# Two attention layers, a gated FFN, a convolution and state space mixer, cross attention and an FFN in one kernel: segment sums by DMA instead of matmul, and five changes of order

## The reference, cut to what matters

```python
# one layer's attention (8 heads of 64, one key and one value head)
proj = rms_norm(x, g) @ w_in            # q, k, v, gates, index queries and keys, ...
score = sum_h(relu(q_idx[h] @ k_idx.T) * w_idx[h])       # w_idx is 8 columns beside v
sel = the 64 best visible keys of each query
p = softmax(where(sel, q @ k.T / 8, -inf));  out = p @ v

# mixer, state space half (32 heads of 64, 4 groups, state 128, chunks of 128)
xbc = silu(causal_dwconv(xbc, conv_w) + conv_b)          # 4 taps, 3072 channels
dt = softplus(dt_raw + dt_bias);  acs = cumsum(dt * a)   # per head, per chunk
decay = exp(acs[l] - acs[s]) for s <= l                  # 128 x 128 per head and chunk
y = (C @ B.T * decay) @ (x * dt) + exp(acs) * (C @ state)
```

## Time and profile before

| | |
|---|---|
| three executions | 1267.33, 1271.03, 1271.29 us, median 1271.03 |
| the profiled execution | 1270.99 us |
| its span | 1269.2 us |
| mean granted clock of TensorE | 0.995 of full speed |
| VectorE, ScalarE, POOL busy | 48%, 56%, 77% of the span |
| chain that ended last | TensorE 91%, VectorE 4%, ScalarE 2%, issue 1%, DMA 1% |
| HBM read, written | 206.07 MB, 1.05 MB |
| mean busy share of the DMA queue of the weights | 49.2% |

### The profile page before, as it was taken

One profiled execution on the slowest core, in us unless ns is written; L12 is line 12 of the kernel. 1 busy time (PEld: TensorE's weight loads), 2 busy tenths in 40 slices (PEclk: granted clock), 3 DMA queues, 4 the chain that ended last, 5 costly groups with the idle time before them and its releaser, 6 DMA issues.

```text
span 1269.2 us, 22533 instructions
## 1 busy us (share of the span) xinstructions
PE 1241.6 (98%) x8950; PEld 1141.5 (90%) x8950; DVE 609.7 (48%) x1489; ACT 716.0 (56%) x1347; POOL 978.8 (77%) x774
## 2 busy tenths in 40 slices
PE   6999999999999999999999999999999999999997
PEld 5899899998889888889999999999999888888886
DVE  4476754456656444422755666632135234444312
ACT  5455656465556666545554676674447446666532
POOL 4567658767568999989799766769889767899894
PEclk9999999999999999999999999999999999999999
DMA  6334335444345555555465444445556434555552
GB/s 233 124 126 158 131 129 183 152 148 150 117 135 192 188 183 190 190 181 186 150 200 200 150 134 136 151 147 180 179 176 223 157 125 157 184 190 191 173 194 81
DMA packets 57784, 208.58 MB, mean 164 GB/s; under 512 B 6352, under 2 KB 7632, under 8 KB 57552
## 3 DMA queue, kind: packets, MB, share of 16 engines
q1 hardware_dynamic: 57680, 207.15, 49.2%
HBM read 206.07 MB, written 1.05 MB: 163 GB/s over the span
## 4 chain that ended last, share of the span: by engine, by line
PE 91%; DVE 4%; ACT 2%; issue 1%; DMA 1%; SPq 0%; POOL 0%; DVEq 0%
PE bank L385 22%; PE bank L358 17%; PE bank L360 16%; PE bank L359 16%; PE bank L388 11%; PE bank L895 1%; PE bank L699 1%; PE bank L1789 1%; ACT whi L310 1%; PE bank L905 1%; DMA raw<-w_dram 1%; PE bank L2166 1%; PE bank L2138 1%; PE bank L837 1%; PE bank L2188 1%
## 5 line engine op out<-in xcount | busy, mean ns | idle before, releaser
L318 POOL TENSOR_TENSOR wlo<-raw,whi 128x512 fp32r<-128x512 f32 x770 | 978.6, 1300 | 275.1 <-ACT whi L310 273.3
L310 ACT ACTIVATE whi<-raw 128x1024 fp32r<-128x1024 f32 x387 | 404.3, 1053 | 33.5 <-DMA raw<-w_dram 11.8
L358 PE MATMUL bank<-xx,whi 128*128 128x256 f32 (+1 forms) x1296 | 378.9, 292 | 12.0 <-DVE xx L448 9.4
L360 PE MATMUL bank<-xx,wlo 128*128 128x256 f32 (+1 forms) x1296 | 368.8, 285 | 0.0
L359 PE MATMUL bank<-xx,whi 128*128 128x256 f32 (+1 forms) x1296 | 368.6, 284 | 0.0
L358 PEld LDWEIGHTS bank<-xx,whi 128*128 128x128 f32 x1296 | 246.4, 190 | 21.3 <-issue 11.7
L360 PEld LDWEIGHTS bank<-xx,wlo 128*128 128x128 f32 x1296 | 246.8, 190 | 0.0
L359 PEld LDWEIGHTS bank<-xx,whi 128*128 128x128 f32 x1296 | 246.3, 190 | 0.5
L385 PE MATMUL bank<-xx,whi 128*128 128x512 f32 x704 | 178.9, 396 | 0.0
L358 PE MATMUL bank<-yy,whi 128*128 128x256 f32 (+1 forms) x524 | 151.2, 289 | 0.0
L360 PE MATMUL bank<-yy,wlo 128*128 128x256 f32 (+1 forms) x524 | 148.9, 284 | 0.0
(11 more groups left out here) (276 smaller groups left out, 1412.8 us busy)
## 6 DMA issues: line engine op xcount, KB each, us to landing
raw<-w_dram SPq DMA_DIRECT2D x387, 512.0 KB, 3.3
h<-x_dram SPq DMA_DIRECT2D x2, 544.0 KB, 6.2
ar<-mem_dram SPq DMA_DIRECT2D x1, 1024.0 KB, 5.6
out_dram<-h SPq DMA_DIRECT2D x4, 256.0 KB, 2.2
cst<-con_dram SPq DMA_DIRECT2D x1, 721.0 KB, 9.6
cst<-con_dram SPq DMA_DIRECT2D x1, 134.0 KB, 3.4
prm<-par_dram SPq DMA_DIRECT2D x1, 131.0 KB, 3.2
```

Of the source, the lines that this page charges most:

```text
L310: e.activation(whi[:, i % NSPL, :], raw[:, i % NRAW, :], ACT.Copy).then_inc(*whi_done.done(i))
L318: return e.tensor_tensor(wlo[:, q, c0:c1], raw[:, i % NRAW, c0:c1], whi[:, q, c0:c1].bitcast(F), ALU.subtract)
L358: e.matmul(o, wh, both[:, 0, :], start=(i == 0), stop=False)
L360: m = e.matmul(o, wl, both[:, 0, :], start=False, stop=(i == len(feed) - 1))
```

## The change

The segment sums come by DMA: `acs` goes to a DRAM tensor of 32 by 256 (`sums`), and each pair of heads is read back from it with both rows spread over all 128 partitions (256 KB in SBUF), into one of three buffers `runs`, 16 loads in all, issued on ScalarE's queue. `E` is then made from that buffer into `E8`, ahead of the wait for the Relus, and the product with `C` is made in place in `E8`. The matmuls `seg`, `acr` and `idr` are gone. `taps` runs block by block, without interleaving; ScalarE has the tanh of the block before (`due`) ahead of its tick. In `attend_scalar` the copies stand ahead of the exponentials. In layer 0 the values' block precedes the keys'. `values_vector` yields six times instead of two.

```diff
 def values_vector(e, K):
         e.tensor_tensor(x[0:72, :], main.at("v", l)[0:72, 0:T], K.N.row[0:72, :], ALU.mult).then_inc(*v_out.done("v", l))
-        yield
-        yield
+        for _ in range(6):
+            yield
         w = K.V[:, 0:2, 64:72]
...
 def attend_scalar(e, K, t):
         for s in range(8):
-            for hh in (2 * s - 2, 2 * s - 1) if 1 <= s < 5 else ():
-                e.wait_ge(*v_step.of("max", l, t, s - 1))
-                e.activation(K.L[:, hh, 0:nk], K.L[:, hh, 0:nk], ACT.Exp, bias=K.nm[:, hh:hh + 1],
-                             accum_out=K.sm[:, hh:hh + 1]).then_inc(*s_step.done("exp", l, t, hh))
             for hh in (2 * s - 6, 2 * s - 5) if 3 <= s < 7 else ():
...
                 e.activation(pt[:, 1:nn, :], o[:, 128:128 * nn].rearrange("p (a b) -> p a b", b=128), ACT.Copy).then_inc(
                     *s_out.done("pt", l, t, hh))
+            for hh in (2 * s - 2, 2 * s - 1) if 1 <= s < 5 else ():
+                e.wait_ge(*v_step.of("max", l, t, s - 1))
+                e.activation(K.L[:, hh, 0:nk], K.L[:, hh, 0:nk], ACT.Exp, bias=K.nm[:, hh:hh + 1],
+                             accum_out=K.sm[:, hh:hh + 1]).then_inc(*s_step.done("exp", l, t, hh))
             yield
...
 def layer_tensor(e, K):
-        block(e, ("kk", l, 0), "w_in", l, [(512, 64, 0), (2688, 64, 64)], K.x_all, T, by=[(v_step, ("rope", l, "kk", 0))])
         if l:
+            keys_tensor(e, K)
             norm_sums(e, N)
         block(e, ("v", l), "w_in", l, [(576, 64, 0), (2752, 8, 64)], K.x_all, T)
         if l == 0:
+            keys_tensor(e, K)
             norm_sums(e, N)
...
+    def load_run(e, n):
+        if n < 16:
+            if n >= 3:
+                e.wait_ge(*s_step.of("fall", *divmod(n - 3, 4)))
+                e.wait_ge(*s_step.of("E", *divmod(n - 3, 4)))
+            e.dma_start(runs[n % 3], sums[2 * n:2 * n + 2, :].partition_broadcast(128)).then_inc(sems[f"run{n % 3}"], 16)
...
 def steps_scalar(e):
         e.wait_ge(*v_step.of("acs", 1))
+        e.dma_start(sums, acs).then_inc(sems["l_a"], 16)
         e.activation(dq[:, 0:128], acs[:, 0:128], ACT.Exp, scale=-1.0, bias=acs[:, 127:128]).then_inc(*s_step.done("dden"))
         yield
...
-        e.activation(acr[0:32, :], acs, ACT.Copy).then_inc(*s_high.done("acr"))
-        for i in (0, 1):
-            e.activation(idr[32 * i:32 * i + 32, :], ident[0:32, 0:32], ACT.Copy).then_inc(*s_high.done("idr", i))
+        e.wait_ge(sems["l_a"], 16)
+        for n in range(3):
+            load_run(e, n)
...
 def ssd_tensor(e, g):
         for hp in range(4):
-            o = side_.take(e, "seg", g, hp)
-            side_.give(("seg", g, hp), (v_step, ("EC", g, hp)))
-            e.wait_ge(*v_low.of("acr"))
-            for i in range(2):
-                hd = 8 * g + 2 * hp + i
-                m = e.matmul(o[:, S * i:S * i + S], idr[:, hd:hd + 1].broadcast_to([64, 128]), acr, start=True, stop=True)
-            m.then_inc(*piece.done("seg", g, hp))
             yield
...
 def ssd_vector(e, g):
                 e.wait_ge(*s_step.of("E", g, hp - 1))
-                e.tensor_tensor(E8[:, 2 * hp - 2:2 * hp, :], later(side_.at("seg", g, hp - 1)), ctb, ALU.mult).then_inc(
-                    *v_step.done("EC", g, hp - 1))
+                m = E8[:, 2 * hp - 2:2 * hp, :]
+                e.tensor_tensor(m, m, ctb, ALU.mult).then_inc(*v_step.done("EC", g, hp - 1))
...
 def ssd_scalar(e, g):
-            o = side_.at("seg", g, hp)
-            e.wait_ge(*piece.of("seg", g, hp))
+            n = 4 * g + hp
+            o = runs[n % 3]
+            e.wait_ge(sems[f"run{n % 3}"], 16 * (n // 3 + 1))
...
-            rise = later(o)
+            e.activation(E8[:, 2 * hp:2 * hp + 2, :], o[:, :, 128:256], ACT.Exp).then_inc(*s_step.done("E", g, hp))
             e.wait_ge(*s_step.of("fall", g, hp))
-            e.activation(rise, rise, ACT.Exp).then_inc(*s_step.done("E", g, hp))
             e.activation(M[:, 2 * hp:2 * hp + 2, :], M[:, 2 * hp:2 * hp + 2, :], ACT.Exp, scale=-1.0).then_inc(
                 *s_step.done("M", g, hp))
+            load_run(e, n + 3)
             yield
...
 def mixer_vector(e):
                     silu_vector(e, due)
                     due = ()
                     tick(side)
-                taps(e, pair)
-                due = pair
+                    taps(e, cb)
+                    due = (cb,)
...
 def mixer_scalar(e):
                     split_for(e, "cv", cb)
+                    silu_scalar(e, due)
+                    due = (cb,)
                     tick(side)
-                    silu_scalar(e, due)
-                    due = ()
-                due = pair
```

More of the change, by code:

```diff
@@ L227, in tick, with build @@
             side.remove(g)
-def build(tens, sems, known, wts, small, par, con, mem, out):
+def build(tens, sems, known, wts, small, par, con, mem, out, sums):
     P, V, A, G, Y = Tensor("pe"), Vector("dve"), Scalar("act"), Pool("pool"), Sync("sp")
@@ L1198, in mixed_low, with keys_tensor @@
                                ALU.subtract).then_inc(*v_low.done("mixed", l, g))
+    def keys_tensor(e, K):
+        l = K.l
+        block(e, ("kk", l, 0), "w_in", l, [(512, 64, 0), (2688, 64, 64)], K.x_all, T, by=[(v_step, ("rope", l, "kk", 0))])
     def layer_tensor(e, K):
@@ L1504, in build @@
     dtu, dtv, dtw = (M[0:32, i, :] for i in (0, 1, 2))
-    acr, idr = tens["acr"][:, 0:S], tens["acr"][:, S:S + 32]
+    runs = [sg[:, 2 * k:2 * k + 2, :] for k in range(3)]
     cwh, cbh, snh = (prm[:, PARAMS[n]:PARAMS[n] + w] for n, w in (("cw", 96), ("cb", 24), ("sn", 16)))
@@ L1691, in short_scalar, with taps @@
         e.activation(yc(16 + j)[0], main.at("ab", j)[:, S:2 * S], ACT.Copy).then_inc(*s_high.done("ya", j))
[L1695 to L1699, removed]
-        for i in range(3):
[L1701 to L1710, removed]
+    def taps(e, cb):
+        s, o = cv.take(e, cb), main.at("cv", cb)
+        cv.give((cb,), (v_out, ("cv", cb)))
+        bias = cbh[:, cb:cb + 1]
+        e.wait_ge(*product.of("cv", cb))
+        e.tensor_scalar(s[:, 0:3], o[:, 0:3], 0.0, bias, ALU.mult, ALU.add).then_inc(*v_step.done("bias", cb))
+        for i in range(3):
+            d, w = 3 - i, cwh[:, 24 * i + cb:24 * i + cb + 1]
+            if i == 0:
+                e.tensor_scalar(s[:, d:S], o[:, 0:S - d], w, bias, ALU.mult, ALU.add).then_inc(*v_step.done("tap", cb, i))
+            else:
                 e.wait_ge(*v_step.of("tap", cb, i - 1))
@@ L1713, in taps @@
                     *v_step.done("tap", cb, i))
[L1714 to L1718, removed]
+        e.wait_ge(*v_step.of("tap", cb, 2))
+        e.scalar_tensor_tensor(o[:, S:2 * S], o[:, 0:S], cwh[:, 72 + cb:73 + cb], s, ALU.mult, ALU.add).then_inc(
+            *v_out.done("cv", cb))
     def silu_scalar(e, cbs):
@@ L1892, in ssd_vector @@
         yield
-    def later(o):
-        return o.rearrange("p (a s) -> p a s", a=2)[:, :, 128:256]
     def ssd_scalar(e, g):
@@ L2414, with program @@
           "wlo_done"]
-LOADS = ["l_h", "l_h2", "l_c1", "l_c", "l_p", "l_m", "o"] + [f"w{i}" for i in range(NRAW)]
-def program(nc, wts_shape_decl, small, par, con, mem, out):
+LOADS = ["l_h", "l_h2", "l_c1", "l_c", "l_p", "l_m", "l_a", "run0", "run1", "run2", "o"] + [f"w{i}" for i in range(NRAW)]
+def program(nc, wts_shape_decl, small, par, con, mem, out, sums):
     with ExitStack() as ctx:
@@ L2428, in program @@
             "cst": sb("cst", [128, NCONST]), "prm": sb("prm", [128, NPARAM]), "ar": sb("ar", [128, ARENA]),
-            "acr": sb("acr", [64, S + 32], R), "sq": sb("sq", [128, 2, T]), "rows": sb("rows", [128, 2, T]),
+            "sq": sb("sq", [128, 2, T]), "rows": sb("rows", [128, 2, T]),
             "banks": [ctx.enter_context(nc.psum_tensor(f"bank{i}", [128, 512], F)) for i in range(8)],
         }
-        plan, counted, engines = build(tens, sems, None, None, small, par, con, mem, out)
+        plan, counted, engines = build(tens, sems, None, None, small, par, con, mem, out, sums)
         for name in ("tensor", "vector", "scalar", "pool", "sync"):
@@ L2435, in program @@
         nslots = -(-len(plan) // TILES)
-        _, _, engines = build(tens, sems, counted(), wts_shape_decl(nslots), small, par, con, mem, out)
+        _, _, engines = build(tens, sems, counted(), wts_shape_decl(nslots), small, par, con, mem, out, sums)
         block = ctx.enter_context(nc.Block())
```

16 lines of the change are left out of this document (7 added, 9 removed).

## The result

The changed kernel takes **1257.6 us** (median of 4 runs, 1255.06 to 1258.27); the kernel before took 1270.82 beside it (4 runs, 1267.33 to 1271.29). The ratio is 0.990 with a 95% interval of 0.988 to 0.992, 1.0% faster. The profiled execution took 1257.13 us, its span is 1255.3.

The account below looks back on a forecast made before the run. TensorE, busy 1241.6 of 1269.2 us, was taken as the bound. Terms 8.8 + 2.1 + 1.4 + 1.1 - 1.2 = 12.2 us, off 1270.99, gave 1258.8 us, range 1254.6 to 1266.0.

Parts of the forecast that it names:

- the side that had 0.88: Whole kernel: the chance given to a faster result was 0.88, within 0.3% 0.06, slower 0.06.
- Part 1: Mixer: removing the `seg` matmuls takes 8.8 us off TensorE, 0.59 a pair in its own tick, 0.43 beside the state product.
- Part 2: Layer 0: the 2.1 us wait for line 722 goes, and 1.4 us of slower clock with it.
- the wait goes, the fall stays: Rival in layer 0: the wait goes but the fall of the clock stays, 1260.2; chance 0.12.
- Part 3: `attend_scalar`: copies ahead of exponentials remove line 895's waits in two places for line 931's copy, 1.1 us.
- Part 4: ScalarE and DMAs in the mixer: the store of `acs`, the loads and their issues cost nothing on the path.
- Part 5: VectorE and main banks: TensorE waits 0.4 us at block 6 in each of three mixer groups, 1.2 us back.
- Line 866's wait: Layer 1: this wait of 1.4 us stays, since nothing VectorE does ahead of it is moved.
- The slower rival: Mixer groups 1 to 3: VectorE becomes the bound, all products held, a group 6.5 us too long, 1281.3; chance 0.05.

Follow-up runs that it names:

- experiment 1: All of the change's orders, but segment sums by matmul as in the kernel before: 1265.22 us, ratio 0.9967 to the kernel before.
- experiment 4: The changed kernel with the first tap of each block done twice, 0.53 us more VectorE time a block: 1266.04 us.
- experiment 6: The changed kernel with the first tap of each block done twice and `E` written to a PSUM bank: 1263.22 us.
- experiment 9: The changed kernel with `attend_scalar`'s exponentials ahead of the copies, as before: 1258.07 us, ratio 0.9909 to the kernel before.
- experiment 2: The changed kernel, but taps in pairs and the tanh behind ScalarE's tick, as before: 1267.47 us, ratio 0.9981 to the kernel before.
- experiment 3: The changed kernel, but taps interleaved in pairs again, the tanh still ahead of ScalarE's tick: 1262.82 us, ratio 0.9938 to the kernel before.

## Why the prediction was right, point by point

1258.8 was predicted, 1257.6 came, within the range and on the side that had 0.88. The mechanism is right in parts 1, 3 and 4; that the total came within 1.2 us owes something to errors that cancel. The parts:

- **Part 1, matmuls: 8.8 predicted, 9.8 measured** (experiment 1: 2.46 in each of four groups; 8.9 net of what part 5 gives back). Pricing a pair by the distance of starts, not by its 0.50 of duration, is what brought this near, and 0.59 for a pair in its own tick is right within 0.02: (2.46 - 0.63) / 3 = 0.61. The term that was too small is the pair beside the state product, worth 0.63 and not 0.43: before, 1.60 us lie between that product and the next block's second matmul (0.95 + 0.43 + 0.22), after it 0.97 (739.05 to 740.02). Four times 0.2 is most of the 1.0 missed.
- **Part 2, layer 0: 2.1 + 1.4 predicted, 2.5 seen.** The wait of 2.1 went. Of the clock, one fall went and another came at 25 to 30, so that the net was 0.4. The rival "the wait goes, the fall stays" (0.12, 1260.2) describes this execution better than the forecast does. In the profiles of experiments 1, 4 and 6, whose layer 0 is that of the changed kernel, the clock falls in neither place, and the stretch that took 54.66 us before and 52.27 here takes 50.77: 3.9 less than before, of which 3.5 were forecast. So the term depends on the execution. The estimate that the embedding ends at 31.3 was wrong: it ends at 32.9, because the keys' block itself is one later; nothing hung on it, since the block that needs the bank starts at 35.39.
- **Part 3: 1.1 predicted, 1.1 seen** (0.4 and 0.7 in the stages; experiment 9 brings back 1.1 of waits).
- **Part 4: nothing, and nothing seen.** Store and loads show no wait of ScalarE. The store is issued at 638.94, the first load at 644.83, 5.9 us later; the loads land in 3.9. ScalarE's busy time around three pairs is 10.1 of 10.4 us as before, and no split came late in the groups.
- **Part 5: 1.2 us back predicted, 1.0 came, but not where the sum had it.** The forecast was 0.4 of wait for a main bank at block 6 in three groups. No such wait came; the room is 0.4 there and 0.3 at block 9. What came is 0.48 at the end of each of two groups, where TensorE pauses for the matmuls that take `M` and for line 1803, and it goes with `E` in PSUM. So the size was luck: the cause (products with `C` that are held) was right and the path was wrong. At block 6 the room was put at 0.9, less 1.3 for `yt` products taken at their mean. Those ahead of block 6 in this group were free (0.75 a pair, as in the kernel before), so that 1.3 was no cost; and the two products with `C` took 0.42 + 1.52 = 1.94 ahead of it, 1.1 more than 2 x 0.417, against 0.7 taken. 0.9 - 0.4 = 0.5 of room, near the 0.4 that is read there. The mean of the product is 813 where 751 was taken. Taking a mean for instructions that are either free (0.42) or held (1.52) made the error; the rows said free in the very group that I was costing. That VectorE was the narrow place, as the sum had it, is shown by experiments 2 to 4: 0.53 us more for each block cost 8.4 us.
- **Line 866's wait** stays at 1.42, as forecast. The fall of the clock behind it was absent in the profiled execution, a gain of 1.5 us that the sum doesn't have.

So 12.2 was forecast for the profiled execution and 13.9 came: + 1.0 from the matmuls, + 0.2 for what was given back, + 0.4 in the mixer beside (the order of taps and tanh, experiment 1), - 1.0 in layer 0, + 1.5 of clock in layer 1, - 0.4 of clock at the end of the span. The three terms of the clock differ from one execution to the next and say nothing of the change.

The slower rival (VectorE the bound, 1281.3) asked for all products to be held. VectorE is busy for 30.6 us of a group, not 37.8. It would have come closer had taps and tanh been left alone: experiment 2 is that case, and it gives away 9.9 us.

## What to carry to other kernels

Work taken off the engine that bounds a kernel is worth the distance of starts that it made, and only if the engine behind it can follow (here the removal alone would have gained nothing): remove and reorder together, and find the room by a dose, not by the share of busy time (49% here, with 0.3 us to spare in the stretch that counts). Where an instruction has two distinct durations, look at which one it has at the place in question and ask what another engine does at that moment; a mean is right for neither. A view of waits has a smallest size: compare starts over a whole stretch before saying that nothing was lost. And a small VectorE step ahead of a TensorE wait is worth a look at its operands: moving one to PSUM took 1.0 us off each of two of them and a wait of 1.8 off TensorE.

## What the runs showed of the hardware

- **The same wait is followed by a fall of the clock in one execution and not in another.** Twelve profiled executions (of the kernel before and eleven others) have the idle time of 1.6 to 1.8 us before line 528 near 24; in seven of them the granted clock falls behind it (to 0.66 between 25 and 30 in the changed kernel), in five it doesn't. Behind the 1.4 us for line 866 near 309 it falls in nine of fourteen. Where it falls, about 1.5 us are lost (320.18 - 312.62 = 7.56 with, 315.76 - 309.72 = 6.04 without). That is the size of the steps between runs of one kernel: those of the changed one span 3.2 us, and the dose with `E` in PSUM took 1260.24 with no fall in its profile ahead of the end where its other runs took up to 1264.4. The start varies as well: in the same twelve executions that matmul of line 528 starts anywhere from 23.78 to 25.61, with the same program ahead of it. A term for the clock should be written with a chance, and one profiled execution can't settle it.
- **VectorE is also held with a single SBUF input.** Line 1277 above scales 128 x 4 elements by a constant and takes 1.15 us, while POOL runs, where the changed kernel's line 1276 takes 0.15 at a moment when POOL is between two instructions. In the attention, line 956 (one tile and a column of scalars) has

```profile
L956 DVE TENSOR_SCALAR ar<-ar x32: 282/561/1397, 117.5 to 356.7; 128x144 f32<-128x144 f32 x16, 128x272 f32<-128x272 f32 x16
```

  The Trainium skill (SBUF — State Buffer, Who interferes with whom) says that such instructions can run in a mode that uses the shared interface too, and the trace agrees: of two of them that stand at 308.03 right ahead of line 866's wait, the first takes 1.02 us, until about where an instruction of POOL ends (307.69 + 1.27 = 308.96), and the second 0.28. That they cause the wait was not tried.
- **The broadcast loads are cheap here.** 16 loads, each spreading two rows of 1 KB over 128 partitions, 256 KB in SBUF, landed in 3.9 us beside the weight stream and took 0.33 us each to issue. The store ahead of them (32 KB) landed in 3.4.
